# Key pages in an eight-page ring, nine value slots, value and gate-weight loads on ScalarE's queue, and another order of the first loads

## The reference

```python
h = rms_norm(x, norm_mix)
q, k, v, u, ga, gp = jnp.split(h @ w_in, SPLITS, axis=-1)
o = attention_fn(q, k, v, lam)           # 8 heads, two 64-d components, 128-d values
merged = sigmoid(ga) * (o @ w_attn_branch) + sigmoid(gp) * (pool_o @ w_pool_branch)
x1 = x + merged @ w_out                  # then a conv FFN on x1

def sample_attention(...):               # per sample: 8 past pages of 128 keys, plus the 8 new keys
    k_past = k_cache[layer, page_table]  # a page is 128 rows of 4 KB (all heads)
    v_past = v_cache[layer, page_table]
    s = concat([q @ k_past, q @ k_new]) * scale
    p = softmax(s[..., 0]) - lam * softmax(s[..., 1])
    return p[:n_past] @ v_past + p[n_past:] @ v_new
```

## Time and profile before

| | |
|---|---|
| time, median of 3 runs | 2114.14 us (2108.64 to 2119.16) |
| profiled execution, its own time | 2115.86 us |
| its span (first to last instruction) | 2114.1 us |
| TensorE matmuls (PE) | 2055.5 us busy, 97% |
| TensorE weight loads (PEld) | 1863.8 us, 88% |
| VectorE (DVE), ScalarE (ACT), GpSimd (POOL) | 1117.7, 608.3, 496.7 us |
| bytes moved by DMA | 189.18 MB |

### The profile page before, as it was taken

One profiled execution on the slowest core, in us unless ns is written; L12 is line 12 of the kernel. 1 busy time (PEld: TensorE's weight loads), 2 busy tenths in 40 slices (PEclk: granted clock), 3 DMA queues, 4 the chain that ended last, 5 costly groups with the idle time before them and its releaser, 6 DMA issues.

```text
span 2114.1 us, 35690 instructions
## 1 busy us (share of the span) xinstructions
PE 2055.5 (97%) x14393; PEld 1863.8 (88%) x14393; DVE 1117.7 (53%) x1471; ACT 608.3 (29%) x1200; POOL 496.7 (23%) x373
## 2 busy tenths in 40 slices
PE   9999999998887989999999999999999999999999
PEld 8888888886775757999999988999999999999997
DVE  6766666664542333266553443554555555555556
ACT  5444445443311111224112422311221122122120
POOL 5333232421111111242331111311221121122120
PEclk9999999999998989999999999999999999999999
DMA  5222212114388786311224320211110111012112
GB/s 150 57 62 57 61 46 56 37 52 122 120 282 286 252 297 210 97 40 50 87 80 124 118 97 11 70 31 41 50 60 12 61 50 41 31 50 61 31 40 96
DMA packets 190791, 189.18 MB, mean 89 GB/s; under 512 B 21536, under 2 KB 164396, under 8 KB 190516
## 3 DMA queue, kind: packets, MB, share of 16 engines
q1 hardware_dynamic: 175660, 176.53, 26.3%
q10 hardware_dynamic: 14992, 10.62, 1.6%
HBM read 162.73 MB, written 24.62 MB: 89 GB/s over the span
## 4 chain that ended last, share of the span: by engine, by line
PE 93%; DMA 3%; SPq 2%; DVE 1%; issue 1%; POOL 0%; ACT 0%; POOLq 0%; DVEq 0%
PE PS L1488 39%; PE PS L2255 13%; PE PS L1016 6%; PE PS L2010 4%; PE PS L282 4%; PE PS L284 4%; PE PS L283 4%; PE PS L338 3%; PE PS L362 3%; DMA v_pg<-in_cache_v_dram 2%; PE PS L1098 2%; PE PS L351 2%; PE PS L1131 1%; PE PS L1509 1%; PE PS L1521 1%
## 5 line engine op out<-in xcount | busy, mean ns | idle before, releaser
L1475 POOL TENSOR_TENSOR fw_lo<-fw_raw,fw_hi 128x1024 fp32r<-128x1024 f32 x86 | 214.6, 2495 | 823.5 <-ACT fw_hi L1471 823.5
L1488 PE MATMUL PS<-m_hi,fw_hi 128*128 128x384 f32 (+1 forms) x1032 | 228.3, 329 | 0.0
L1488 PE MATMUL PS<-m_lo,fw_hi 128*128 128x384 f32 (+1 forms) x1032 | 227.5, 328 | 0.0
L1488 PE MATMUL PS<-m_hi,fw_lo 128*128 128x384 f32 (+1 forms) x1032 | 227.5, 328 | 0.0
L2383 DVE TENSOR_TENSOR x<-x,PS 128x512 f32<-128x512 f32 x198 | 136.2, 688 | 143.6 <-PE PS L2255 143.3
L1488 PEld LDWEIGHTS PS<-m_hi,fw_lo 128*128 128x128 f32 x1032 | 176.3, 188 | 0.0
L1488 PEld LDWEIGHTS PS<-m_lo,fw_hi 128*128 128x128 f32 x1032 | 176.3, 188 | 0.0
L1488 PEld LDWEIGHTS PS<-m_hi,fw_hi 128*128 128x128 f32 x1032 | 176.0, 188 | 0.4 <-POOL fw_lo L1475 0.2
L282 PE MATMUL PS<-w_hi,act_hi 128*128 128x384 f32 (+1 forms) x456 | 164.7, 361 | 0.0
L284 PE MATMUL PS<-w_hi,act_lo 128*128 128x384 f32 (+1 forms) x456 | 153.6, 337 | 0.0
L283 PE MATMUL PS<-w_lo,act_hi 128*128 128x384 f32 (+1 forms) x456 | 153.1, 336 | 0.0
(11 more groups left out here) (316 smaller groups left out, 4235.0 us busy)
## 6 DMA issues: line engine op xcount, KB each, us to landing
k_ring<-in_cache_k_dram SPq DMA_DIRECT2D x64, 512.0 KB, 5.7
v_pg<-in_cache_v_dram SPq DMA_DIRECT2D x56, 512.0 KB, 6.3
fw_raw<-in_w_up_dram SPq DMA_DIRECT2D x44, 512.0 KB, 3.9
fw_raw<-in_w_in_dram SPq DMA_DIRECT2D x24, 512.0 KB, 4.7
wd_raw<-in_w_down_dram SPq DMA_DIRECT2D x22, 512.0 KB, 4.4
w_raw<-in_w_in_dram SPq DMA_DIRECT2D x21, 512.0 KB, 5.2
out_dram<-raw SPq DMA_DIRECT2D x16, 512.0 KB, 3.7
sa_ring<-ga_scratch SPq DMA_DIRECT2D x8, 544.0 KB, 3.6
```

Source lines behind the costliest of these rows:

```text
L1475: e.tensor_tensor(fw_lo[slot][:, 0:kts, :], fw_raw[:, 0:kts, :], fw_hi[slot][:, 0:kts, :].bitcast(F32), ALU.subtract).then_inc(fw_tail, 1)
L1488: ins = e.matmul(PS[:, 3 * slot + c, 0:cw], w[slot][:, kt, :], x[:, kt, c0:c0 + cw], start=first and kt == 0, stop=last and kt == KT - 1)
```

## The change

1. `k_ring` has 8 pages, in page order; all eight keys of sample b + 1 are asked for after `sc_full` of sample b.
2. There are 9 value slots. A page's load is asked for by ScalarE (`act_load_values`) in sample b's list, four behind chunk 1 and four behind chunk 2; values of all samples use these slots.
3. `fm_load` in phase 2 (and for the chunks p = 3 and 6 in the last head) stands in ScalarE's `act_chunk`, right behind the copy of the chunk with c = 0, with its wait for `fw_tail`.
4. The stores of a sample's output move from ScalarE's list to SyncE's (but the last sample's).
5. First loads: four key pages come first, then the stores of head 7, then three key pages, the queries, two value pages; the eighth key page waits for the last matmul of phase 1 and for the stores, no longer for the copy and the store of the output. VectorE turns four pages in the last head, in steps 5 to 8.
6. The chunks are dealt out as 6, 5, 4, 4, 4, 4, 3, 2 to the samples; sample 0's first chunk stands ahead of its scores.

```diff
-                if not proj and 1 <= s <= KEYS_TURNED_EARLY:
-                    dve_turn_keys(e, s - 1)
+                if not proj and s > QT - KEYS_TURNED_EARLY:
+                    dve_turn_keys(e, s - QT + KEYS_TURNED_EARLY - 1)
-        KEY_GROUP = NPG // 2
-        RK = 3 * KEY_GROUP
+        HALF = NPG // 2
+        RK = NPG
+        mid_pg = [r(f"v_pg{j}", [P, NH * VD]) for j in range(2, 6)]
-        KEYS_TURNED_EARLY = KEYS_EARLY // 2 * 2
+        KEYS_TURNED_EARLY = 4
-        late_pg = [r(f"v_pg{j}", [P, NH * VD]) for j in range(2, 5)]
+        late_pg = [r(f"v_pg{j}", [P, NH * VD]) for j in range(6, 9)]
-        P_PER = (NC * N_FILL - TT - 1) // NB
+        P_EACH = (6, 5, 4, 4, 4, 4, 3, 2)
...
             e.activation(dst, PS[:, PJ + use % 2, 0:cw], ACT.Copy).then_inc(pj_free, 1)
             if c == NC - 1 and n + 2 <= N_U:
                 fm_head(e, n + 2, n % 2)
+            if c == 0 and n >= 1 and n + 2 <= N_U:
+                fm_load(e, n + 2, gate_cols(n + 2) if n + 2 < N_U else w_in_cols(COL_U))
...
+        def act_load_values(e, b, first, last):
+            for g in range(RV + b * NPG + first, min(RV + b * NPG + last, NB * NPG)):
+                load_values(e, g)
...
                 act_chunk(e, fill[1])
-                if b:
-                    act_stores(e, b - 1)
-                act_chunk(e, fill[2])
+                act_load_values(e, b, 0, HALF)
+                for p in fill[2:3]:
+                    act_chunk(e, p)
+                act_load_values(e, b, HALF, NPG)
                 act_take_values(e, b)
...
-            e.wait_ge(k_ld[g % RK // 2], 32 * (g // RK + 1))
+            e.wait_ge(k_ld[g % RK // HALF], HALF * 16 * (g // RK + 1))
...
             e.wait_ge(pj_full, NH * TT)
-            for g in range(2):
-                sp_load_values(e, g)
-            sp_store_kv(e, NH - 1, 1)
             e.wait_ge(b7_free, b_use(NH - 2, True, ("o", TT - 1)) + 1)
             e.wait_ge(kv_st[0], NH // 2 * 64 + 1)
-            for g in range(KEYS_EARLY):
+            for g in range(HALF):
+                sp_load_keys(e, g)
+            sp_store_kv(e, NH - 1, 1)
+            for g in range(HALF, KEYS_EARLY):
                 sp_load_keys(e, g)
...
-            for p in range(TT):
-                sp_chunk(e, p)
-            phase1_over(e)
+            for g in range(2):
+                load_values(e, g)
+            e.wait_ge(b7_full, b_use(NH - 1, False, ("o", TT - 1)) + 1)
+            e.wait_ge(kv_st[1], NH // 2 * 64 + 1)
             sp_load_keys(e, KEYS_EARLY)
             for g in range(2, RV):
-                sp_load_values(e, g)
-            for g in range(KEYS_EARLY + 1, RK):
-                sp_load_keys(e, g)
+                load_values(e, g)
...
             for b in range(NB):
                 e.wait_ge(sc_full, b + 1)
+                for g in range((b + 1) * NPG, min(b + 2, NB) * NPG):
+                    sp_load_keys(e, g)
                 if b + 2 < NB:
                     e.wait_ge(qb_ready, b + 1)
                     sp_load_queries(e, b + 2)
+                if b:
+                    store_outputs(e, b - 1)
```

More of the change, by code:

```diff
@@ L957, in build_step @@
         r = Region(RING, R3)
-        v_pg = [r(f"v_pg{j}", [P, NH * VD]) for j in range(2)] + late_pg
+        v_pg = [r(f"v_pg{j}", [P, NH * VD]) for j in range(2)] + mid_pg + late_pg
         RV = len(v_pg)
@@ L962, in build_step @@
         pg_ld = sem("pg_ld")
-        k_ld = [sem(f"k_ld{j}") for j in range(RK // 2)]
+        k_ld = [sem(f"k_ld{j}") for j in range(RK // HALF)]
         v_ld = [sem(f"v_ld{j}") for j in range(RV)]
@@ L988, in build_step @@
         P_FIRST = TT
-        P_PER = (NC * N_FILL - TT - 1) // NB
-        assert TT + 1 + NB * P_PER == NC * N_FILL
+        P_EACH = (6, 5, 4, 4, 4, 4, 3, 2)
+        assert TT + 1 + sum(P_EACH) == NC * N_FILL and len(P_EACH) == NB
         def chunks_of(b):
-            p = P_FIRST + 1 + b * P_PER
-            return range(p, p + P_PER)
+            p = P_FIRST + 1 + sum(P_EACH[:b])
+            return range(p, p + P_EACH[b])
         ga_dram = nc.dram_tensor("ga_scratch", [P, N_SPILLED, TOK], F32, kind="Internal").ap()
@@ L1051, in pool_chunk @@
                 e.wait_ge(fw_tail, n + 3)
-        def sp_chunk(e, p):
-            n, c = divmod(p, NC)
-            if c == 0 and n >= 1 and n + 2 <= N_U:
-                fm_load(e, n + 2, gate_cols(n + 2) if n + 2 < N_U else w_in_cols(COL_U))
         def phase1_over(e):
@@ L1064, in phase1_over @@
                 e.wait_ge(kv_st[i], NH // 2 * 64 + 1)
-        def key_groups(b):
-            first, second = 2 * b % 3, (2 * b + 1) % 3
-            return min(first, second), max(first, second), first > second
-        def page_block(b, j):
-            half, i = divmod(j, KEY_GROUP)
-            return (1 - half if key_groups(b)[2] else half) * KEY_GROUP + i
         def queries(g, r, x, part):
@@ L1079, in pe_scores_of_sample @@
         def pe_scores_of_sample(e, b):
-            lo, hi, _ = key_groups(b)
-            pages = k_ring[:, :, :].rearrange("p (g j) n -> p g j n", j=KEY_GROUP)[:, lo:hi + 1:hi - lo, :, :]
             e.wait_ge(qb_ready, b + 1)
@@ L1098, in pe_scores_of_sample @@
                             ins = e.matmul(PS[g * QB:(g + 1) * QB, B_S + i, 0:2 * P], queries(g, r, x, part),
-                                           pages[part, :, :, c:c + QB], start=r == 0 and x == 0, stop=r == 1 and x == XB - 1)
+                                           k_ring[part, :, c:c + QB], start=r == 0 and x == 0, stop=r == 1 and x == XB - 1)
             ins.then_inc(sc_full, 1)
@@ L1105, in pe_probs @@
             for j in range(NPG):
-                ins = e.matmul(PS[:, B_PTS, j * NH * NS:(j + 1) * NH * NS], es[:, page_block(b, j) * PAGE:][:, 0:PAGE],
+                ins = e.matmul(PS[:, B_PTS, j * NH * NS:(j + 1) * NH * NS], es[:, j * PAGE:(j + 1) * PAGE],
                                pick_r[b % 2][:, :], start=True, stop=True)
@@ L1122, in pe_value_page @@
                 v = v_new
-            elif b == NB - 1:
-                e.wait_ge(k_ld[(END_SLOT + j) // 2], 32 * (NB * NPG // RK + 1))
-                v = k_ring[:, END_SLOT + j, :]
             else:
@@ L1145, in pe_phase2, with store_output @@
                 fill = [lambda p=p: pe_chunk(e, p, {}) for p in chunks_of(b)]
+                if b == 0:
+                    fill[0]()
                 pe_scores_of_sample(e, b)
-                fill[0]()
+                if b:
+                    fill[0]()
                 fill[1]()
                 pe_probs(e, b)
-                for j in range(KEY_GROUP):
+                for j in range(HALF):
                     pe_value_page(e, b, j)
-                fill[2]()
-                for j in range(KEY_GROUP, NPG + 1):
+                for f in fill[2:3]:
+                    f()
+                for j in range(HALF, NPG + 1):
                     pe_value_page(e, b, j)
-                fill[3]()
-        def act_store(e, b, par, h):
+                for f in fill[3:]:
+                    f()
+        def store_output(e, b, par, h):
             e.dma_start(o_dram[bass.ds(SEQ + b * NS, NS), h * VD:(h + 1) * VD],
@@ L1273, in sp_load_keys, with load_values @@
         def sp_load_keys(e, g):
-            sp_load_page(e, g, k_ring[:, g % RK, :], k_ld[g % RK // 2], cache_k)
-        def sp_load_values(e, g):
+            load_page(e, g, k_ring[:, g % RK, :], k_ld[g % RK // HALF], cache_k)
+        def load_values(e, g):
             if g >= RV:
                 e.wait_ge(v_used, g - RV + 1)
-            sp_load_page(e, g, v_pg[g % RV][:, :], v_ld[g % RV], cache_v)
-        def sp_load_last_values(e, j):
-            sp_load_page(e, (NB - 1) * NPG + j, k_ring[:, END_SLOT + j, :], k_ld[(END_SLOT + j) // 2], cache_v)
+            load_page(e, g, v_pg[g % RV][:, :], v_ld[g % RV], cache_v)
         def sp_load_queries(e, b):
```

37 lines of the change are left out of this document (10 added, 27 removed).

## The result

The changed kernel takes 2087.91 us (median of 4 runs, 2086.4 to 2089.52); before takes 2113.79 in the runs beside it. The ratio is 0.9877, 95% interval 0.9852 to 0.9903: 26 us faster, where 46 (2114 to 2068) were forecast. 2087.9 lies just inside the range given (2053 to 2088), beyond the likeliest case's own 2055 to 2078 and inside rival 1's 2079 to 2089. The profiled execution took 2089.52 us, its span is 2087.7, 26.4 less than before.

The account below looks back on a forecast made before the run. PE, busy 97% of the span, was taken as the bound, with 58.6 us idle. The terms -12.4 + 6 - 5.8 - 36 = -48 from 2115.9 us gave 2068 us, range 2053 to 2088.

Parts of the forecast that it names:

- likeliest case: Whole kernel: the forecast of 2068 us holds, with a time of 2055 to 2078 us; chance 0.67.
- rival 1: Samples: the DMA engines become the bound and idle until keys can be asked for; 2079 to 2089 us, chance 0.22.
- Keys turned in steps 5 to 8: Last head, at 503 us: PE's wait behind a key turn and the slow clock there go; -12.4 us.
- The weight load on ScalarE: Last head: ScalarE waits for tile 2's tail before loading tile 3's weights, delaying the copies behind; +6 us.
- Start of the samples: From chunk 9 to the first value page: the wait for turned keys goes, at most 1 us left; -5.8 us.
- I keep it: Start of the samples: PE's one "issue" wait of 2.68 us stays, as the pages in flight do.
- Nine value slots and eight key pages: Samples 1 to 6: waits for value pages go, less what late keys and "issue" waits take back; -36 us.
- 5 us over all samples: Samples: allowance for keys that can be asked for only after the scores; 5 us, from 0 to 17.
- 1.5 for 'issue' waits that stay: Samples: 1.5 us allowed for "issue" waits that remain, of some 2 us in the scores.
- about T0 + 14: Samples: all eight key pages land some 14 us after the scores end (T0), leaving four us of margin.
- Rivals 2 and 3: At 503 us PE waits for more than the turn, 2074 to 2080, 0.06; or ScalarE becomes the bound, 0.05.
- Rival 3: Samples: page loads hold ScalarE x us each; no faster or slower, 2126 us at x = 4.0; chance 0.05.

Follow-up runs that it names:

- e1: Kernel before with only its six turns of key pages moved to steps 3 to 8 of the last head; 2108.67 us, ratio 0.9977.
- e2: Kernel after with the weights of tiles 3 and 4 asked for by SyncE behind the queries; 2077.46 us, ratio 0.9829.
- e6: Kernel after with the value loads on SyncE's queue behind keys and queries, same nine slots; 2090.25 us, ratio 0.9891.
- e8: e2 with the last four value pages of a sample asked for behind its own scores; 2088.8 us, ratio 0.9887.
- e9: e8 with four chunks in each sample; 2086.85 us, ratio 0.9882.
- e13: e2 with a chunk inside the scores of samples 1 to 7, two chunks behind them, all nine value products in one run; 2084.76 us, ratio 0.9861.
- e10: e2 with all nine value products in one run, the chunk between moved behind, eight value loads in one run; 2079.8 us, ratio 0.9841.
- e11: e10 with four chunks in each sample; 2082.56 us, ratio 0.986.
- e5: Kernel before with 2 MB copied from DRAM to DRAM beside it in each sample but the last; 2139.82 us.
- e12: Kernel after without value pages from the tenth on and without key pages of samples 1 to 7; 2067.76 us.

## Why the prediction was right in direction and wrong in size

**Keys turned in steps 5 to 8, -12.4.** Measured 12.7, clock included. e1 adds what the prediction didn't see: done alone, this step gives back half of it to a query load that is then the next to be late.

**The weight load on ScalarE, +6.** Right place and mechanism, undersized: 9.4. The prediction had the tail of tile 2 late by 1.6 us against the chunks. The tail's end was 533.48 for a chunk 2 that ended at 520.10, 13.4 us behind it; now it is 525.10 + 2.34 = 527.44 for 509.35, 18.1 us behind. 3.1 of these 4.7 us are the eight query stores, which take 8.18 us right behind key loads where they took 5.10. e2 shows the whole cost and that it was avoidable: 10.4 us.

**Start of the samples, -5.8.** Measured -3.4: 28.00 us in place of 31.40. The wait for keys is gone as forecast. "I keep it" of the one issue wait of 2.68 us was too little: there are two, 2.62 and 1.80.

**Nine value slots and eight key pages, -36.** This is the step that was mis-sized. The first half of it held: every wait for `v_pg` is gone, and e6 shows that slots did it. The other half, "5 us over all samples" for what the keys take back and "1.5 for 'issue' waits that stay", was too small. The trace of before has 3.0 us of such waits already, and nothing in the working says why 1.5 should stay. The seven score stages last 65.9 us; clean ones at 6.4 with those 6.5 us would be 51.3. That is 14.5 us, and with the 2.4 of sample 0's start it is the whole shortfall behind the start of chunk 9: 294.7 us before (563.5 to 858.15), 252.9 forecast (41.8 less), 269.75 measured. The kernel that loads no pages has 251.75. So the forecast was, to 1 us, that of a kernel whose page traffic costs nothing, and traffic costs 18. The keys, too, came later than "about T0 + 14": VectorE gets the second four of them 17.1 to 20.5 us behind the end of the scores, in sample 2 at 673.86 for an end at 653.36. That uses up the four us of margin, and TensorE waits 0.87 and 1.79 us, in samples 3 and 7 alone.

**Rival 1, the DMA engines become the bound.** Its time came out, 2079 to 2089, and so in a sense did its cause: the engines are busy for 0.75 to 0.83 of samples 1 to 6, and of the other arrangements tried, e8, e9 and e13 turned one wait into another, while e10 and e11 kept it. Its mechanism, keys asked for late, is not where the time went: waits for `k_ring` are 2.7 us in all. That the time lies in the stated range, which was widened for this rival, is luck more than reasoning.

**What the unexplained waits are.** Where the time went is TensorE's instruction supply. The trace has a queue for it, q8: 109 packets, 1.79 MB, 16.4 KB each, all of one size (16384 bytes). The Trainium skill, "Runtime: NRT & Kernel Launch", section "Instruction fetch mechanics", says that each sequencer fetches blocks of 16 KiB, 256 instructions, over a DMA queue of its own. Size and distance agree, and so does the number: 109 x 256 = 27904, and TensorE has 28786 matmuls and weight loads. The packets can be placed in time. In sample 3's wait of 682.88 to 686.33 us there is one, in the second of these two windows of the DMA view (682.88 to 683.80 and 683.80 to 684.90):

```profile
q10 hardware_dynamic: 320, 0.18, 61.6%
...
q10 hardware_dynamic: 99, 0.05, 14.9%
q8 instruction: 1, 0.02, 5.6%
```

Read packet by packet (us from the span's start; a block is 256 of TensorE's matmuls and weight loads, counted off from one stop to the next; the DMA share is that between its entry and the start of the packet):

| | block entered | DMA share | next block's packet | matmuls go on | stop |
|---|---|---|---|---|---|
| after, sample 2 | 648.49 | 0.00 | 649.59 to 650.67 | 651.95 | 0.71 |
| after, sample 6 | 777.90 | 1.06 | 780.23 to 781.29 | 782.80 | 2.35 |
| after, sample 3 | 680.13 | 0.94 | 683.83 to 684.82 | 686.33 | 3.45 |
| e5, sample 1 | 608.87 | 1.04 | 610.03 to 611.47 | 612.92 | 1.33 |
| e13, sample 4 | 703.60 | 1.03 | 706.40 to 707.51 | 709.90 | none |

So there are three parts. Where a block is entered within the page scores and the DMA engines are idle (a share under 0.1), the next packet starts 0.5 to 1.4 us after that; it takes about 1.0; the matmuls go on 1.3 to 1.6 us after it has landed. In sum that is 3.0 to 3.8 us, and the 256 instructions of the scores are used up in 2.76. They stop for 0.2 to 0.8 us even on idle engines: of the 4.0 us that e12 has left in samples 1 to 7, 1.7 are four such stops. With full engines the start can slip to some 4 us, and the stop grows with it. It is so in every trace: the fourteen traces have 133 "issue" waits of TensorE between 480 and 870 us, every one stands at the same place of the 256 (to one instruction), and 131 of them end 1.2 to 1.6 us after such a packet has landed (the other two, both in e6, 1.0 and 2.3). The 2.68 us of the earlier trace rows are one of them. The skill's section also says that crossing a block is mostly hidden; here that holds for the chunks, whose blocks last longer, and not for the scores, whose blocks last 2.76 us.

The packets also answer for the two experiments that left a doubt. In e13 the packets start as late as before (2.6 to 3.8 us in samples 2 to 6, with the engines full), but with a chunk in the block the next one isn't needed for 6.3 to 9.3 us: it is the pace. In samples 1 and 2 of e5 the one packet that the scores need starts after 1.16 and 0.89 us; the late one (4.0 and 3.0 us) is the next, and its stop falls on the chunk behind, 2.69 and 0.60 us. Full engines don't always delay a packet: in samples 2 and 4 of the kernel after one starts 0.96 and 0.81 us after the block is entered, at shares of 0.99 and 1.03.

**The rule weighed in the prediction.** By the Trainium skill, "DMA: Bandwidth & Descriptors", section "Issuing engines are not separate DMA queues", a second issuing engine brings no bandwidth. e6 agrees: 2090.3 against 2087.9 us within their intervals. I had set 2104 beside this rule as the sum if the queue were all of the change; the slots were the rest.

**Rivals 2 and 3** didn't come. Four value pages are issued in 3.5 us on ScalarE's queue, 0.9 each, and no chunk waits for a copy of ScalarE. Rival 3's "Half way, x = 3.4: within 0.5% of now" is a slip: by its own sum x = 3.4 gives 2068 + 7 x 3.6 = 2093, and no difference begins at x = 3.6.

Open: what makes a packet start after 0.8 us in one place and after 3.7 in another, with the DMA engines full in both. What is queued ahead of it may matter, and no run here separates it. Also open is whether a deeper key ring, which would let keys move earlier, would make e13's order pay; ring and slots hold 17 pages together in both kernels, so it would have to take slots from the values.

## What to carry to other kernels

When a change moves transfers from a stretch where an engine waited for them into one where it works, price what they do there: the densest run of short instructions is the place that suffers, and the profile calls it "issue". Such a wait can be checked: count TensorE's matmuls and weight loads from one to the next (here 256 or a multiple), and look for a packet of the instruction queue that lands just before it ends. Where the DMA engines are busy for 0.8 of a loop, a forecast should take the loop with its loads left out as the floor, not as the result, and expect moved loads to wait for each other. A load with a wait in it does not belong on the queue of an engine that has copies behind it: one that was late cost 10 us here (the second, behind chunk 6, found its tail made), and moving it was worth more than any reordering of pages.

## What was not expected of the hardware

- The same 320 score matmuls take 6.2 to 6.5 us with 5 GB/s moving in e12 (once 7.8, with two stops of 0.5 and 0.7), 6.8 to 7.6 with 76 to 82, and 8.5 to 11.8 with more than 200 in the kernel after, where single stops last up to 3.5 us and two stages have 0.9 and 1.8 us of waits for keys in them.
- TensorE's instructions come in blocks of 256 over the same DMA engines as the pages, and within the page scores the next block's packet starts only after the block before has been entered. There, from that entry to the first matmul of the next block, it took 3.0 to 3.8 us on idle engines and 6.2 in sample 3 of the kernel after; a block of scores lasts 2.76 us.
- Such a stop also costs the clock. After the 3.45 us of sample 3 the granted clock is 0.50, 1.2 in place of 2.4 GHz, up to 690 us and back at 1.00 from 692 on; the chunk behind pays for it too. In the stages of samples 3, 5, 6 and 7 PE is busy 7.5 to 8.0 us for work of 6.06.
- Eight small stores on SyncE's queue are issued in 5.10 us with nothing issued in the seven microseconds ahead of them, and in 8.18 right behind three key pages; in e1, right behind seven, in 8.75.
